# Differential attention ordered by sequence and head, with the score maps mixed before they are normalised, and mLSTM decay rows fetched by DMA

## What is computed

```python
def mlstm_chunkwise(q, k, v, log_i, log_f):     # here in one chunk per sequence
    logD = where(tri, b[t] - b[s] + li[s], -inf); m_t = maximum(inter, max(logD))
    sc = (q @ k.T) * exp(logD - m_t)            # decay matrix, rows depend on -m_t
...
def diff_attention(q, k, v, lam):
    s = jnp.einsum('bqhmd,bkhmd->bhmqk', qblk, k).astype(F32) * scale   # m: two maps
    p = jax.nn.softmax(s, axis=-1)
    a = p[:, :, 0] - lam * p[:, :, 1]
    return jnp.einsum('bhqk,bkhe->bqhe', a.astype(v.dtype), v)
...
o_c = (rms_norm(o_c, c_hn_g) * (1.0 - lam_init)).reshape(Bn, S, C_WIDTH)
mixed = gates[:, :, 0] * y_a + gates[:, :, 1] * y_b + gates[:, :, 2] * y_c
x = x + mixed @ w_out
```

## Time and profile before

| | us |
|---|---|
| median of three runs | 3615.83 |
| lowest and highest run | 3612.37, 3620.4 |
| the profiled execution | 3621.54 |
| its span, first to last instruction | 3619.9 |
| TensorE busy | 3258.0 (90%) |
| VectorE busy | 1596.1 (44%) |
| ScalarE busy | 1164.2 (32%) |

### The profile page before, as it was taken

How to read it: one execution, slowest core, us unless ns; L and a number is a source line. 1 busy time by engine, 2 the same in 40 slices (tenths; PEclk the granted TensorE clock), 3 DMA queues, 4 the chain that set the end, 5 groups by cost and what they waited for, 6 DMA issues and landing times. The chain is left out here.

```text
span 3619.9 us, 45917 instructions
## 1 busy us (share of the span) xinstructions
PE 3258.0 (90%) x17716; PEld 2952.0 (82%) x17716; DVE 1596.1 (44%) x3321; ACT 1164.2 (32%) x2456; POOL 483.8 (13%) x854
## 2 busy tenths in 40 slices
PE   6899988998876999999978899879988779999998
PEld 6789876887766799999878898768877668999997
DVE  5345256453345334434453442564434453344434
ACT  4334423554422221111143334235553222121111
POOL 0111311211233000000001114112112220000000
PEclk9899998999997999999988999999999979999999
DMA  3434433333455122112043344333335551222111
GB/s 128 132 98 132 129 126 98 112 91 99 145 141 162 47 70 70 54 50 70 30 131 96 104 132 126 125 101 105 94 100 156 131 169 35 66 70 70 54 50 64
DMA packets 273050, 358.60 MB, mean 99 GB/s; under 512 B 27128, under 2 KB 209592, under 8 KB 272856
## 3 DMA queue, kind: packets, MB, share of 16 engines
q1 hardware_dynamic: 214520, 182.59, 17.0%
q0 software_dynamic: 58336, 173.45, 15.5%
HBM read 261.27 MB, written 94.69 MB: 98 GB/s over the span
## 5 line engine op out<-in xcount | busy, mean ns | idle before, releaser
L1648 PE MATMUL ps<-wh,xh 128*128 128x384 f32 (+1 forms) x1536 | 579.3, 377 | 19.3 <-DVE wl L1259 6.6
L1649 PE MATMUL ps<-wl,xh 128*128 128x384 f32 (+1 forms) x1536 | 563.8, 367 | 0.0
L1650 PE MATMUL ps<-wh,xl 128*128 128x384 f32 (+1 forms) x1536 | 563.7, 367 | 0.0
L1259 DVE TENSOR_TENSOR wl<-wraw,wh 128x1024 fp32r<-128x1024 f32 (+2 forms) x210 | 232.3, 1111 | 429.0 <-ACT wh L1000 429.0
L1648 PE MATMUL ps<-xh,wh 128*128 128x384 f32 (+1 forms) x1056 | 374.0, 354 | 38.2 <-DVE ol L1345 14.9
L1718 PE MATMUL ps<-xh,wh 128*128 128x384 f32 x1408 | 361.1, 337 | 20.1 <-DVE arena L1635 15.3
L1649 PE MATMUL ps<-xl,wh 128*128 128x384 f32 (+1 forms) x1056 | 360.3, 341 | 0.0
L1650 PE MATMUL ps<-xh,wl 128*128 128x384 f32 (+1 forms) x1056 | 360.2, 341 | 0.0
L1718 PE MATMUL ps<-xl,wh 128*128 128x384 f32 x1408 | 359.0, 336 | 0.0
L1718 PE MATMUL ps<-xh,wl 128*128 128x384 f32 x1408 | 358.8, 335 | 0.0
L1648 PEld LDWEIGHTS ps<-wh,xh 128*128 128x128 f32 x1536 | 299.0, 195 | 55.1 <-DVE ol L1345 7.1
(11 more groups left out here) (211 smaller groups left out, 5315.8 us busy)
## 6 DMA issues: line engine op xcount, KB each, us to landing
wraw<-in_w_in SPq DMA_DIRECT2D x96, 512.0 KB, 4.1
wraw<-in_w_ffn_in SPq DMA_DIRECT2D x88, 512.0 KB, 4.0
wraw<-in_w_in SPq DMA_DIRECT2D x72, 384.0 KB, 3.4
wraw<-in_w_ffn_out SPq DMA_DIRECT2D x44, 512.0 KB, 3.4
qkv_a<-stage POOLq DMA_DIRECT2D x108, 192.0 KB, 2.2
gate_t<-stage POOLq DMA_DIRECT2D x96, 192.0 KB, 2.2
stage<-gate_t POOLq DMA_DIRECT2D x96, 192.0 KB, 2.8
mix_t<-stage POOLq DMA_DIRECT2D x64, 192.0 KB, 3.8
```

Source lines behind the costliest of these rows:

```text
L1259: dve.tensor_tensor(wl[:, half, j, 0:w], wraw[:, n % RAW, 0:w], wh[:, half, j, 0:w].bitcast(F32), ALU.subtract).then_inc(w_lo, 1)
L1648: pe.matmul(out, ah, bh, start=first, stop=False)
L1649: pe.matmul(out, ah, bl, start=False, stop=False)
L1650: return pe.matmul(out, al, bh, start=False, stop=last)
```

## The change

C's units are ordered by sequence and head, the long sequence first. One head's q, k and v are loaded at a time into two-fold buffers (`load_c`, `load_cv`), in place of one tile of all heads, and `c_fold` transposes one head, in two halves for the long sequence. `c_score` leaves only the negated maximum and the exponentials; a new step `c_mix` on VectorE follows one place later and combines the two maps without normalising them, one scaled add in place of four instructions. The normalising by the first map's sum moves to `c_norm`, which now comes once for each head (eight times) and reads the head's results straight from PSUM; the 24 copies of L1567 go. A place in the list holds up to `c_mix` of u-1, `c_score` of u, `c_turn` of u-2, `c_out` of u-3, `c_norm` and a `c_fold`. The gap before each place is 4 instead of 5. The last row tiles turned are those of the short sequence (`TURN_ORDER`).

In branch B the step `b_decay` leaves TensorE. `b_columns` stores `nmx` to memory, waits until it has landed, and loads units 0 and 1 spread over all partitions; later units are loaded at `b_conv`. VectorE and ScalarE read those rows from SBUF instead of PSUM.

```diff
-GAP_A, GAP_B, GAP_C, ROUND = (1, 2, 4, 2.5), (4, 6, 4), (4, 5), 0.45
+GAP_A, GAP_B, GAP_C, ROUND = (1, 2, 4, 2.5), (4, 6, 4), 4, 0.45
...
-C_UNITS = [(s, t, h) for s, (t0, n) in enumerate(SEQS) for t in range(n) for h in range(C_H)]
+C_HEADS = [(s, h) for s in (1, 0) for h in range(C_H)]
+C_UNITS = [(H, t) for H, (s, h) in enumerate(C_HEADS) for t in range(SEQS[s][1])]
...
-        for i in range(m + 2):
-            if i < m:
-                order.append((("c_score", u0 + i), GAP_C[1]))
-            if 1 <= i <= m:
-                order.append((("c_turn", u0 + i - 1), 0 if i < m else 5))
-            if i >= 2:
-                order.append((("c_out", u0 + i - 2), 0 if i < m else 3))
-                if (i - 2) % C_H == C_H - 1:
-                    order.append((("c_norm", p0 + (i - 2) // C_H), 0))
...
+    for u in range(m + 3):
+        slot = []
+        if 1 <= u <= m:
+            slot.append(("c_mix", u - 1))
+        if u < m:
+            slot.append(("c_score", u))
+        if 2 <= u < m + 2:
+            slot.append(("c_turn", u - 2))
+        if u >= 3:
+            slot.append(("c_out", u - 3))
+            if u - 3 in C_LAST:
+                slot.append(("c_norm", C_LAST.index(u - 3)))
+        if u < m:
+            H, t = C_UNITS[u]
+            if H + 1 < len(C_HEADS):
+                slot += c_folds(H + 1)[t:t + 1]
+        order += [(x, 0 if i else GAP_C) for i, x in enumerate(slot)]
...
+TURN_ORDER = [tuple(range(NT))] * 2 + [(2, 3, 4, 5, 0, 1)]
...
+                    def load_decay(u):
+
+                        s, h = B_UNITS[u]
+                        t0, n = SEQS[s]
+                        if u >= 2:
+                            pool.wait_ge(b_dec, u - 1)
+                        pool.dma_start(b_nb[:, u % 2, :, 0:n * P], nmx_d[:, h, t0 * P:(t0 + n) * P].partition_broadcast(P)
+                                       ).then_inc(b_nbin[u % 2], 16)
...
-                        if p == 0:
-                            pool.wait_ge(b_store, 16 * len(B_UNITS))
-                            pool.dma_start(c_e[:, 0, 0:4 * HD], io["c_lambda"][layer].rearrange("a b -> (a b)")
-                                           .partition_broadcast(P)).then_inc(c_lamin, 16)
-                        else:
-                            pool.wait_ge(c_tr, p)
-                        if t == 0 and s == 1:
-                            pool.wait_ge(c_pv, SEQS[0][1] * C_H)
-                        pool.dma_start(c_in.rearrange("p (i n) -> p i n", i=2), qkv_c[rows, 0:2, :]
-                                       ).then_inc(c_lin, 16)
-                        pool.dma_start(c_v[:, t, :], qkv_c[rows, 2, :]).then_inc(c_vin, 16)
...
+                        if H >= 2:
+                            pool.wait_ge(c_tr, C_FOLDS.index(c_folds(H - 2)[-1]) + 1)
+                        for i in range(2):
+                            pool.dma_start(c_in[:, H % 2, i, 0:n, :], qkv_c[rows, i, h * P:(h + 1) * P].rearrange(
+                                "(t p) e -> p t e", p=P)).then_inc(c_lin[H % 2], 16)
...
+                            pool.wait_ge(bg_scan, 4)
+                            pool.dma_start(nmx_d.rearrange("d h n -> h d n"), nmx[0:4, :, :]).then_inc(nmx_out, 16)
                             pool.wait_ge(bg_cols, 2)
+                            pool.wait_ge(nmx_out, 16)
+                            load_decay(0)
+                            load_decay(1)
...
-                            load_c(0)
+                            pool.wait_ge(b_store, 16 * len(B_UNITS))
+                            for H in range(2):
+                                load_c(H)
+                            pool.dma_start(c_e[:, 0, 0, 0:4 * HD], io["c_lambda"][layer].rearrange("a b -> (a b)")
+                                           .partition_broadcast(P)).then_inc(c_lamin, 16)
+                            for H in range(2):
+                                load_cv(H)
...
+                            pool.wait_ge(co_n, H + 1)
+                            pool.dma_start(o_tok[1, t0 * P:(t0 + n) * P, h * P:(h + 1) * P].rearrange(
+                                "(t p) e -> p t e", p=P), c_o[:, H % 2, 0:n, :]).then_inc(c_store[H % 2], 16)
...
-                            if u:
-                                act.wait_ge(c_ptr, u)
-                            for m in range(2):
-                                act.activation(c_e[:, m, 0:n * P], side[:, 512 * m:512 * m + n * P], ACT.Exp,
-                                               bias=unit_s[:, 34 + m:35 + m], scale=HD ** -0.5,
-                                               accum_out=unit_s[:, 36 + m:37 + m]).then_inc(c_ex, 1)
+                            if u >= 2:
+                                act.wait_ge(c_ptr, u - 1)
+                            for m, total in ((0, c_z[:, H % 3, t:t + 1]), (1, c_s[:, u % 4, 2:3])):
+                                act.activation(c_e[:, u % 2, m, 0:n * P], side[:, 512 * m:512 * m + n * P], ACT.Exp,
+                                               bias=c_s[:, u % 4, m:m + 1], accum_out=total).then_inc(c_ex, 1)
...
-                            dve.wait_ge(b_bc, u + 1)
+                            dve.wait_ge(b_nbin[u % 2], 16 * (u // 2 + 1))
+                            if u:
...
-                            chain.link(dve.tensor_reduce(unit_s[:, 32:34], side[:, 0:1024].rearrange(
-                                "p (m n) -> p m n", m=2)[:, :, 0:n * P], AX_X, ALU.max))
-                            dve.tensor_scalar(unit_s[:, 34:36], unit_s[:, 32:34], -HD ** -0.5, None, ALU.mult
-                                              ).then_inc(c_mx, 1)
+                            dve.tensor_reduce(c_s[:, u % 4, 0:2], side[:, 0:1024].rearrange("p (m n) -> p m n", m=2)[:, :, 0:n * P],
+                                              AX_X, ALU.max, negate=True).then_inc(c_mx, 1)
...
+                        elif kind == "c_mix":
+                            u = step[1]
+                            H, t = C_UNITS[u]
+                            n = SEQS[C_HEADS[H][0]][1]
+                            k, e = c_s[:, u % 4, :], c_e[:, u % 2, :, 0:n * P]
                             dve.wait_ge(c_ex, 2 * (u + 1))
-                            chain.link(dve.reciprocal(unit_s[:, 38:40], unit_s[:, 36:38]))
-                            chain.link(dve.tensor_tensor(unit_s[:, 39:40], unit_s[:, 39:40], lam[:, 0:1], ALU.mult))
-                            e0, e1 = c_e[:, 0, 0:n * P], c_e[:, 1, 0:n * P]
-                            chain.link(dve.tensor_scalar(e1, e1, unit_s[:, 39:40], None, ALU.mult))
-                            dve.scalar_tensor_tensor(e0, e0, unit_s[:, 38:39], e1, ALU.mult, ALU.subtract
+                            chain.link(dve.reciprocal(k[:, 3:4], k[:, 2:3]))
+                            chain.link(dve.scalar_tensor_tensor(k[:, 4:5], k[:, 3:4], lam[:, 0:1], c_z[:, H % 3, t:t + 1],
+                                                                ALU.mult, ALU.mult))
+                            dve.scalar_tensor_tensor(e[:, 0, :], e[:, 1, :], k[:, 4:5], e[:, 0, :], ALU.mult, ALU.add
...
-                            dve.tensor_copy(c_o[:, h * P:(h + 1) * P], side[:, 1536:1536 + P]).then_inc(c_ov, 1)
...
+                            chain.link(dve.reciprocal(unit_s[:, 44:44 + n], c_z[:, H % 3, 0:n]))
+                            dve.tensor_tensor(o, side[:, AT_OUT:AT_OUT + n * P].rearrange("p (t e) -> p t e", t=n),
+                                              spread(unit_s[:, 44:44 + n]), ALU.mult).then_inc(c_ov, 1)
...
-                        elif kind == "b_decay":
-                            u = step[1]
-                            s, h = B_UNITS[u]
-                            t0, n = SEQS[s]
-                            if u:
-                                pe.wait_ge(b_h, u)
-                            for d in range(2):
-                                mm = pe.matmul(side[:, 512 * (2 + d):512 * (2 + d) + n * P],
-                                               ident[0:4, h:h + 1].to_broadcast([4, P]),
-                                               nmx[0:4, d, t0 * P:(t0 + n) * P], start=True, stop=True)
-                            mm.then_inc(b_bc, 1)
```

More of the change, by code:

```diff
@@ L297, in schedule @@
     side, gone, since = side_order(), set(), 0
-    late = [("turn_load", 2, 0), ("turn_load", 2, 1)]
-    for t in range(NT):
-        late += [("turn", 2, t)] + ([("turn_load", 2, t + 2)] if t + 2 < NT else [])
+    late = [("turn_load", 2, t) for t in TURN_ORDER[2][:2]]
+    for k, t in enumerate(TURN_ORDER[2]):
+        late += [("turn", 2, t)] + [("turn_load", 2, x) for x in TURN_ORDER[2][k + 2:k + 3]]
     loaded_at = {}
@@ L304, in schedule @@
             kind, _, t = late[0]
-            free = ("turn", 1, NT - 1) in gone and ("c_norm", t) in gone
+            free = ("turn", 1, NT - 1) in gone and ("c_norm", 3 if t >= SEQS[1][0] else 7) in gone
             if kind == "turn":
@@ L548, in build @@
         b_store = sem("b_store")
-        c_lin = sem("c_lin")
```

(13 more changed lines are left out.)

218 lines of the change are left out of this document (116 added, 102 removed).

## The result

| | before | changed |
|---|---|---|
| median, us | 3619.84 (8 runs) | 3635.47 (8 runs) |
| lowest and highest | 3612.37, 3625.65 | 3632.79, 3639.86 |
| the profiled execution | 3621.54 | 3634.64 |
| its span | 3619.9 | 3633.0 |
| TensorE busy | 3258.0 | 3221.7 |

The account below looks back on a forecast made before the run. TensorE was taken to bound the gates, POOL's store queue the mixes. Per layer -3.7 + 5.6 + 2.7 + 20.3 - 31.1 = -6.2 us, -12.4 in all: 3603 us against the median of 3615.8, range 3582 to 3628.

Parts of the forecast that it names:

- Part 1, long units: Branch B's long units without `b_decay`: freed 1.9 us become TensorE's wait, gain 0 (bounds 0 and 7.6), 0.5 us loss for ScalarE.
- Part 1, short units: Branch B's short units without `b_decay`: an earlier gate product shortens the loop, 4 x 1.05 = 4.2 us gained a layer.
- Part 2, the head of B: Start of branch B: store of `nmx`, landing and two loads delay `conv_in`; +5.6 us a layer (bounds 2 and 9).
- Part 3, the head of C: Start of branch C: four loads now stand ahead of the four vectors; +2.7 us a layer (bounds 1 and 6).
- Part 4, the gates: Branch C among the gates: longer units there, less idle, plus a new loop of +6.0 us; +20.3 us a layer.
- Part 5, the mixes: Mix stores through `wout`: first store sooner, shorter early intervals, shorter end; -31.1 us a layer (bounds -37 and -19).
- The end: Last mix store to `wout`: loads and `branch 2` start sooner because POOL's queue is shorter; -26.6 us a layer.
- The next 15: Mix-store intervals after the first 16: the last head's `c_norm`, store and turn load stand in POOL's queue; +1.8 us.
- The second: Rival, first mixes: POOL held by the norms of short heads, 11.4 us a layer more, 3626 us; chance 0.16.
- the loops don't bind: Rival, gates: they stay TensorE-bound and `conv_in`'s delay is half as long; 7 us a layer more gained, 3589 us; chance 0.22.
- the end gives less: Rival, end: `branch 2` bound by loads of sum and gates; 8.4 us a layer less gained, 3620 us; chance 0.12.
- the lower clock cost more in the late mixes: Rival: short bursts in later mixes lower TensorE's clock, lasting into `branch 2`; 25 us a layer, 3653 us; chance 0.03.

Follow-up runs that it names:

- `conv_in` first: The changed kernel with the first conv_in loaded before POOL waits for the decay rows' store: 3620.6 us, ratio 1.0009 to the kernel before.

## Why the prediction was wrong

**Part 1, long units: the step that failed.** The prediction let "the freed 1.9 us turn into that wait" and priced the longer wait at nothing but 0.5 us. The wait did grow, from 1.1 to 3.5 us, and the loop of VectorE and ScalarE grew by 0.3 us (25.0 to 25.3 a unit). All waits ahead of `b_out` make 25.5 us, where 15 were named as the sign. What was left out is what TensorE does behind a wait of that length: its clock goes to the lower level, between 1.3 us before and 1.4 us behind its first product, and the first thing that it runs is `b_out`, which is in the loop. That costs 7.4 and 4.3 us in the two layers, 11.7 in all, and no bound of part 1 had it. The fact itself was in part 2, where the slow products behind a 5.75 us wait were counted; it was not carried over to the wait that part 1 makes. The products that add work again and give 10.8 us back show it.

**Part 1, short units.** Forecast -4.2, measured -1.5 and -2.1. The step is right, and the miss comes from outside it: the slow start behind the wait ahead of `b_qk 0` falls into this row. With `conv_in` first, which has no such wait, the row is -4.4 and -3.9, though the waits of 1.0 and 3.05 us ahead of the last short `b_out` and the first long one are the same.

**Part 2, the head of B.** Right: the row has 3.6 and 3.7 us, but it ends where `b_qk 0` starts, and the slow start behind it costs another 2.9 and 1.8 us, 6.5 and 5.5 in all for the forecast's 5.6. Inside it the store took 3.4 and 3.66 us and not 2.1, `conv_in` was issued 4.8 and 5.0 us later, but landed faster (5.4 and 4.7 us from issue to VectorE, 5.8 and 5.9 in the kernel before), where 1 us was added for shared transfers. The slow start was put at 1 us. The bounds of 2 and 9 don't follow from the store's ends, which give 3.5 and 8.2.

**Part 3, the head of C.** Forecast +2.7, measured +5.1 and +4.2. The queue's term was right (2.98 us), but the four vectors' load went out 4.2 us later behind the last `b_out`. Of the rest, 1.1 us is the store of the last head: POOL issued it 1.4 us behind VectorE's last instruction, where it was 0.3, and the profile names no cause. In layer 1 the four vectors also needed 0.95 us longer. By the Trainium skill's page "DMA: Bandwidth & Descriptors" (the anatomy of a gpsimd DMA) the four vectors would land 2.3 us after issue, an estimate from its figures; the trace has 4.32, so taking the row was right.

**Part 4, the gates.** Right: +18.0 and +19.7 for +18.3 with the first store's 2 us. The loop waits at `c_score` in this stretch are 6.5 us a layer, at seven places, where 6.0 at seven were forecast. The four places that were moved cost 3.5 us each, where work and loop were put at 3.3.

**Part 5, the mixes: the second step that failed.** The end was right (-25.8, -25.1 for -26.6). The first 16 intervals gained 2.8 and 1.0 for 4.3, in a row that varies by 7 us; their mean over those ten kernels is 66.5 us, and 68.5 in the two with the old order, so about 2 us are gained. The next 15 carry the miss: +1.8 for the last `c_norm`, measured +4.9 and +7.0. The order had been read for POOL, but not for TensorE, where the last `c_out` is queued behind turns that wait for POOL. With the turns behind it, this term is 0.2 to 0.5.

**The rivals.** The second named the place (POOL waits for `c_norm`) and the price too low, 3.8 us, at the first heads; it came at the last one alone. That the loops don't bind, and that the end gives less, did not happen. Nor did the lower clock cost more in the late mixes: it is 0.83 there, with 0.84 in the kernel before:

```profile
2861.00:2945.00 84.00, 51.50 (x236) 48.27 (x236) 16.67 (x28) 6.03 (x10) 24.14 (x35) 0.83 0.50 99
```

The rule on bursts shorter than their waits ("TensorE: Matmul & The Clock Gate", HAM oscillation, of the Trainium skill) was weighed at the mixes, where the rows show no cost. It isn't the rule that decides in branch B: there some 26 us of TensorE's loop of 30 lie between two waits of 3.5 us, and one such wait was enough.

The table's sums are off by 15.6 and 17.1 us. Of these the long units are 7.4 and 4.0, the late intervals 3.1 and 5.2, the first 16 intervals and the short units together 4.2 and 5.4, the head of C 2.4 and 1.5; the gates and the end make 0.5 and 2.9 more, and the head of B 2.0 and 1.9 less. By branch: for C -16.2 us in all were forecast, and with branch B undone it is +3; for B +3.8 were forecast, and alone it costs 12.7. So about 19 us of the 28 between forecast and result are C's, with the late intervals as the largest term (8.3 us) and the others below 5, and 9 are B's, where the low clock in the long units alone is 11.7. Neither of the two failed steps explains the miss by itself: with either one mended the kernel stands at 1.0013 and 1.0017, no faster than before. That the last `c_out` stands behind three turns could have been read from the list of steps.

## What to carry to other kernels

Work that is taken from an engine that already waits in a loop gains nothing, and on TensorE it can cost: look at how long the wait becomes and at what runs first behind it. If that is a part of the loop, leave some work in the gap or put useful work there. A slow start also shows in the stretch behind the one that caused it, so a stretch that misses its forecast is not yet a step that failed. And when a step is placed, read for each engine what it now stands behind: a turn that waits for a load in another engine's queue holds everything that TensorE has behind it, and that queue may be waiting for it. Units belong where another queue sets the time; here each one moved from the gates to the mixes gave 3.5 us.

## What the runs showed of the hardware

- With a wait of 3.04 to 3.53 us TensorE's clock went to its lower level in 35 of 36 cases and came back inside `b_out`; with waits of 2.25 us and less in 1 of 68. The loss was 2.1 us on the mean, 1.4 to 3.0. In 19 of the 35 the clock was still up when `b_out` began, and fell up to 1.4 us later: the wait is paid for behind it.
- Behind waits of 3.8 to 5.2 us ahead of `b_qk 0` the clock of the next 4 us was 0.50 to 0.61 in 12 of 12 cases, and 1.00 in 14 of 14 behind 0.6 us or less.
- A store of 4 rows of 2 x 768 numbers and the wait for its landing held POOL's queue for 3.66 us (3.4 to 4.1 in the six kernels with this order), where a mix store of 192 KB has an interval of 4.7 us: a small store is not a cheap one if something waits for it.
- The same first 593 us, the same instructions, took from 593.1 to 598.5 us in the profiled executions of the 13 kernels.
